# Swapping two blocks of matmuls in the slots of an attention stage: the weighted values ahead of the logits

## What is computed

```
logits = q . k * 64 ** -0.5                       # per head, 1024 x 1024, keys strictly before the query
log_keep = log_sigmoid(-logits)                   # 0 where masked
later = reverse cumulative sum of log_keep over the keys, less log_keep
weights = exp(log_sigmoid(logits) + later)        # 0 where masked
out = weights . v
```

## Time and profile before

| | |
|---|---|
| time, median of 3 runs | 2355.76 us (2354.05 to 2357.71) |
| the profiled execution's own time | 2353.2 us |
| its span, first to last instruction | 2351.4 us |
| TensorE (PE) busy | 2264.8 us, 96% of the span |
| weight loads (PEld) | 1888.8 us, 80% |
| VectorE (DVE) busy | 1603.4 us, 68% |
| ScalarE (ACT) busy | 940.6 us, 40% |
| GpSimd (POOL) busy | 325.7 us, 14% |
| the slots of layer 1's attention | about 59 to 414 us of the span |

### The profile page before, as it was taken

How to read it: one execution, slowest core, us unless ns; L and a number is a source line. 1 busy time by engine, 2 the same in 40 slices (tenths; PEclk the granted TensorE clock), 3 DMA queues, 4 the chain that set the end, 5 groups by cost and what they waited for, 6 DMA issues and landing times. The chain is left out here.

```text
span 2351.4 us, 31886 instructions
## 1 busy us (share of the span) xinstructions
PE 2264.8 (96%) x11464; PEld 1888.8 (80%) x11464; DVE 1603.4 (68%) x2112; ACT 940.6 (40%) x1631; POOL 325.7 (14%) x305
## 2 busy tenths in 40 slices
PE   7999999999999999999999899988999999999997
PEld 6888887888888888887877788877878888888886
DVE  4666768866655456567877878764687777775557
ACT  4443544343333311343444455543433333234443
POOL 0222222000000000002222545430020000000000
PEclk9999999999999999999999999999999999999999
DMA  4111111244333453432234322103324443438654
GB/s 146 45 46 54 46 36 46 90 157 146 104 130 107 169 201 140 143 124 91 98 108 150 96 68 76 57 0 134 119 87 188 156 170 152 156 150 300 218 186 170
DMA packets 105915, 285.94 MB, mean 122 GB/s; under 512 B 9580, under 2 KB 35404, under 8 KB 101324
## 3 DMA queue, kind: packets, MB, share of 16 engines
q1 hardware_dynamic: 105804, 284.46, 34.7%
HBM read 202.32 MB, written 82.10 MB: 121 GB/s over the span
## 5 line engine op out<-in xcount | busy, mean ns | idle before, releaser
L124 PE MATMUL psG<-h_hi,w_hi 128*128 128x512 f32 (+1 forms) x624 | 165.0, 397 | 2.1 <-DVE features_T L1850 1.7
L124 PE MATMUL psG<-h_hi,w_lo 128*128 128x512 f32 (+1 forms) x624 | 161.8, 391 | 0.0
L124 PE MATMUL psG<-h_lo,w_hi 128*128 128x512 f32 (+1 forms) x624 | 161.4, 392 | 0.0
L421 POOL TENSOR_TENSOR sb_w<-sb_left 128x128 f32<-128x128 f32 (+3 forms) x96 | 96.7, 1012 | 298.9 <-DVE sb_left L548 298.9
L124 PEld LDWEIGHTS psG<-h_hi,w_hi 128*128 128x128 f32 x624 | 110.8, 191 | 23.7 <-DVE features_T L1850 2.9
L124 PEld LDWEIGHTS psG<-h_hi,w_lo 128*128 128x128 f32 x624 | 111.6, 189 | 19.9
L124 PEld LDWEIGHTS psG<-h_lo,w_hi 128*128 128x128 f32 x624 | 111.2, 189 | 19.9 <-issue 0.5
L1997 POOL TENSOR_TENSOR features_T<-m_bias_both 128x512 f32<-128x512 f32 x10 | 15.9, 1595 | 681.4 <-DMA m_bias_both<-in_proj_pairs 634.1
L548 DVE TENSOR_TENSOR_SCAN sb_left<-sb_left 128x128 f32<-128x128 f32 (+3 forms) x96 | 102.6, 1076 | 2.1 <-ACT sb_left L434 1.4
L149 ACT CAST w_hi<-w_raw 128x1024 fp32r<-128x1024 f32 x48 | 50.4, 1050 | 119.3 <-PE psG L124 67.1
L154 DVE TENSOR_TENSOR w_lo<-w_raw,w_hi 128x1024 fp32r<-128x1024 f32 x46 | 56.2, 1224 | 55.0 <-ACT w_hi L149 55.0
(11 more groups left out here) (608 smaller groups left out, 6110.4 us busy)
## 6 DMA issues: line engine op xcount, KB each, us to landing
w_raw<-in_units SPq DMA_DIRECT2D x84, 512.0 KB, 3.9
w_raw<-hidden_blocks SPq DMA_DIRECT2D x77, 256.0 KB, 2.9
merge_gates<-features_T SPq DMA_DIRECT2D x12, 1024.0 KB, 7.2
merge_gates<-merge_gates SPq DMA_DIRECT2D x12, 1024.0 KB, 4.9
features<-features_T SPq DMA_DIRECT2D x24, 512.0 KB, 4.4
w_spare<-in_units SPq DMA_DIRECT2D x22, 512.0 KB, 4.2
hidden_blocks<-features_T SPq DMA_DIRECT2D x11, 1024.0 KB, 3.9
down_sums<-w_spare SPq DMA_DIRECT2D x22, 512.0 KB, 3.3
```

The costliest lines, as they stand in the source:

```text
L124: return pe.matmul(out, lhs, rhs, start=first, stop=last, skip_group_check=True)
L421: pool.tensor_tensor(w, left_chunk(S, 1), left_chunk(S), ALU.subtract).then_inc(w_ready, 1)
```

## The change

In TensorE's list of every slot from the third on, the call of `values` is put ahead of the call of `logits`. No instruction is added or removed, no wait is changed, and no other engine's list is touched.

```diff
             for S in range(N_CHUNKS):
                 first, per = FIRST_GROUP[S], PER_SLOT[S // NS]
-                logits(S)
                 if S >= 2:
                     for n in BACKS_AT[S - 2]:
                         values(n)
+                logits(S)
                 projections(first, first + 2)
                 for n in BACKS_AT[S]:
                     turn_weights(n)
```

## The result

The changed kernel takes 2360.0 us in the median of 22 runs (2358.3 to 2362.8), against 2357.5 us for the kernel before, also in 22 runs; the medians differ by 2.5 us. The ratio of the two is 1.0015 with a 95% interval of 1.0009 to 1.0020, which is 2.1 to 4.7 us. The profiled execution's span is 2358.6 us.

What follows compares the result with a forecast made beforehand. TensorE's own list was taken as the bound; 2.04 us and 2.15 us at group starts sum to +4.2 us, so 2360.0 us from a median of 2355.76 us, range 2356.0 to 2363.5 us.

Steps and rivals of the forecast that it cites:

- The chain ahead of gate_add: Projection matmul, evacuation, weight split, move_out, gate_add: 4.0 us in slot 12, not waiting for values, so not brought forward.
- Narrow starts: Group starts with 256-wide logits (slots 13, 25, 37, 49, 73, 85): 0.34 us lost at each, 2.04 us.
- Wide starts: Group starts with 512-wide logits (slots 21, 33, 45, 81, 93): 0.43 us lost at each, 2.15 us.
- The slots without a start: Slots where no group of values begins: same TensorE work in the other order, costed at nothing.
- The free starts: Group starts in slots 57, 61 and 69: gate_add ends before the slot begins, so they cost nothing.
- The signs: Trace marks of a right forecast, among them psO loads waiting in 11 places, some 8 us in total.
- Absorbed: Rival, chance 0.08: VectorE or ScalarE paces gate_add, each wait swallows earlier delays; +0.4 us, 2356.2 us.
- the later `keep`: Rival, chance 0.07: later keep delays ScalarE and VectorE, gate_add 0.47 us later at 14 starts; +10.8 us, 2366.6 us.
- The gain: Rival, chance 0.03: move_out waits for the values, so comes earlier, and keep waits are saved; -1.3 us, 2354.5 us.
- The clock: Rival, chance 0.02: the 11 longer waits each bring TensorE's lower clock, 3.3 us each; +40 us, 2396 us.

Runs made afterwards that it cites:

- the narrow starts alone: Kernel before, with values ahead of logits only at places 1 and 13 of each round (256-wide logits); stretch 330.63 us against 328.48, one run.
- the first experiment: Changed kernel, but logits first again in slots where a group of values can begin; 2356.4 us against 2356.8 for the kernel before, ratio 0.9995.
- slot 13 alone: Kernel before, with values ahead of logits only in slot 13; stretch from slot 7 to slot 95 328.90 us, +0.41, one run.

## Why the prediction was right

**The sign, the size and the place.** 2360.0 us was forecast and measured, though that the two agree to a tenth is luck: the median of the kernel before moved from 2355.8 to 2357.5 us as more runs came in, so that the medians differ by 2.5 us where 4.2 was forecast. The ratio's interval and the stretch's +4.6 us are the better test of the +4.2 us.

**The chain ahead of gate_add** was read rightly: it starts at a TensorE matmul, does not wait for the values, and before ten of the 11 waiting starts it takes the same time after the change, within 0.02 us. Two things about it were not as told. The unit's last projection matmul ended at 102.87, so 0.16 us inside slot 12 and not before it; nothing in the sum hangs on that. And before slot 85 the chain got shorter: `gate_add` starts 3.33 us after slot 84 begins, where it was 3.45, because the weight split ahead of it on VectorE (line 154) took 1.22 us and not 1.33. Why the split was shorter there is open.

**Narrow starts**, 6 x 0.34 = 2.04 us: from the transposes of one slot to those of the next, the changed kernel loses 0.37, 0.37, 0.35, 0.35, 0.36 and 0.22 us at slots 13, 25, 37, 49, 73 and 85, 2.0 us together; with the narrow starts alone 2.1. The 0.12 us by which slot 85 lies below the others are those of the shorter split; with the narrow starts alone the split took 1.33 us, and slot 85 lost 0.34. Here the rows were weighed against the Trainium skill ("TensorE: Matmul & The Clock Gate", Back-to-back issue gap), whose formula gave an estimate of 6 x 0.27 = 1.6 us. The section calls that formula the gap of an isolated matmul and gives 131 ns at 512 columns for a sustained stream; the 512-wide matmuls here are 225 ns and more apart. The measurement takes the side of the rows: the logits of slot 13 take 0.12, 0.12 and 0.06 us, and 0.05 more on the next matmul behind the 128-wide one.

**Wide starts**, 5 x 0.43 = 2.15 us: they lose 0.45, 0.45, 0.46, 0.43 and 0.46 us, 2.25 together. Two small terms were mis-sized, and they pulled against each other: the 0.05 us by which the values were to start earlier, and the 0.03 us by which the next values matmul was to come later. PE's timeline of slot 21 after the change, to be read with the earlier trace rows; `gate_add` ends at 139.84 + 0.68 = 140.52:

```profile
140.62 0.36 PE L124 MATMUL psO<-sb_w_lo,sb_v_both 128*128 128x256 f32 x1 [0.26 <-issue]
...
141.10 0.44 PE L124 MATMUL psA<-sb_k_both,sb_q_hi 128*128 128x512 f32 x1
141.38 0.39 PE L124 MATMUL psA<-sb_k_both,sb_q_lo 128*128 128x512 f32 x1
141.61 1.09 PE L124 MATMUL psG<-h_hi,w_hi 128*128 128x512 f32 x4
```

The values begin 0.10 us after `gate_add`, as at slots 33, 81 and 93 before, and not 0.05. The next values matmul follows after 0.19 us, as before, and not 0.22. Both terms are nothing, and the price is the block of logits alone.

**The slots without a start** were costed at nothing. They cost about 0.35 us together (4.6 less 2.0 and 2.25), and 0.46 in the first experiment. This is the step of the sum that failed: "the same work in the other order" is not quite the same time.

**The free starts** were free: from slot 51 to slot 69 the loss does not grow beyond that small spacing, and at slot 69 `gate_add` is still done 0.21 us before the values begin. The tail is unchanged: its first values wait 0.89 us before the change and after it.

**The signs.** The loads of `psO` were to wait "0.3 to 1.2 us each, some 8 us in total"; they wait 11.8 us, up to 1.9 each. I had counted from the start of the slot's first matmul, but a load is issued a matmul earlier, and in slots 49, 73 and 85 that first matmul had itself been held back by `keep`.

**The rivals.** "Absorbed" fell with slot 13 alone, the later `keep` with the first experiment. The gain did not come, and `move_out` still starts where the split ends (104.77). The clock held. In the profile after, TensorE idled up to 1.4 us at a group start with 1.00 granted; the Trainium skill (same page, section Why this matters for your kernels) warns of the lower clock after long idle gaps between matmuls, and none of these brought it.

**Open:** of the 4.6 us in the slots the totals show 2.1 to 4.7. The two agree within that interval. From the first transpose of slot 95 to the end the profiled execution took 1938.1 us before and 1940.8 after, so this pair shows nothing given back; but over the nine profiled kernels this rest varies from 1938.1 to 1944.1 us, and a small gain in it would not be seen.

## What to carry to other kernels

In an engine's list, what can already run belongs ahead of what must wait, and a wait is judged by when it ends, not by how long it is: the waits for `keep` looked like something to gain, but a later wait in the same slot covered them. If a block that can run stands ahead of one that must wait, swapping the two costs the length of the first, which no longer runs in the shadow of the wait. It costs that once for each wait, and the losses add up if the chain that is waited for starts at the same engine. The larger gain lay on the other engines: moving the short operation that releases the buffer ahead of long ones that nobody waits for yet took 5 us off the kernel, and it made the order nearly irrelevant.

## What was not expected of the hardware

TensorE's time for the same matmuls depends a little on their order. Over the slots of the first experiment the same instructions took 0.46 us more with no wait added. A 128-wide matmul behind a wider one is followed after 0.06 us (107.47 to 107.53), further 128-wide ones behind it after 0.11, and the first wider one behind them is itself followed 0.05 us late (slot 16 before: 0.17 us from the one at 118.98, where other 256-wide ones take 0.12). And the first matmul behind a wait for `gate_add` is followed by the second after 0.22 us at the narrow starts (106.65 to 106.87) and 0.19 at the wide ones, in place of 0.12. So a wait costs more than TensorE's idle time shows: in slot 13 of the kernel before the matmuls show 0.06 us of idling, but with the earlier `gate_add`, which takes this wait away, the distance from the transposes of slot 12 to those of slot 13 is 0.26 us shorter.
